# Moving the first turn of a 96-wide head from attention step 4 into step 5 of a hybrid decoder trunk

## The reference

```python
qb = heads(rms_norm(cq, cq_norm) @ w_uq, B_HEADS)
kv = heads(rms_norm(ckv, ckv_norm) @ w_ukv, B_HEADS)
k_nope, vb = jnp.split(kv, [B_NOPE_DIM], axis=-1)
kb = jnp.concatenate([k_nope, k_rope], axis=-1)
qb = rope_slice(rms_norm(qb, mla_qn), B_NOPE_DIM, B_ROPE_DIM, cos_b, sin_b)
kb = rope_slice(rms_norm(kb, mla_kn), B_NOPE_DIM, B_ROPE_DIM, cos_b, sin_b)
yb = causal_attention(qb, kb, vb)
...
merged = jax.nn.sigmoid(g_a) * (ya @ w_br_a) + jax.nn.sigmoid(g_b) * (yb @ w_br_b)
```

## Time and profile before

| | us |
|---|---|
| median of 3 runs | 1272.4 |
| lowest and highest run | 1271.33, 1274.69 |
| the profiled execution | 1271.69 |
| its span on the core | 1269.9 |
| TensorE busy | 1253.3 |
| VectorE busy | 436.7 |
| ScalarE busy | 381.2 |

### The profile page before, as it was taken

One profiled execution on the slowest core, in us unless ns is written; L12 is line 12 of the kernel. 1 busy time (PEld: TensorE's weight loads), 2 busy tenths in 40 slices (PEclk: granted clock), 3 DMA queues, 4 the chain that ended last, 5 costly groups with the idle time before them and its releaser, 6 DMA issues.

```text
span 1269.9 us, 29364 instructions
## 1 busy us (share of the span) xinstructions
PE 1253.3 (99%) x13480; PEld 890.9 (70%) x13480; DVE 436.7 (34%) x706; ACT 381.2 (30%) x650; POOL 101.0 (8%) x96
## 2 busy tenths in 40 slices
PE   9999999999999989999999999999999999999997
PEld 7877788888889868785555556655665666667666
DVE  5786666554356785652111101110111011101110
ACT  7587836434337678721000000000000000000000
POOL 0220000000001210000001002002001020020011
PEclk9999999999999999999999999999999999999999
DMA  8632535655446524499999999999999999999981
GB/s 300 211 106 100 199 133 185 229 184 197 149 139 227 173 67 166 160 381 424 421 423 422 408 422 402 422 423 394 422 419 404 423 403 417 423 398 423 417 336 16
DMA packets 77108, 379.95 MB, mean 299 GB/s; under 512 B 7786, under 2 KB 14612, under 8 KB 52404
## 3 DMA queue, kind: packets, MB, share of 16 engines
q1 hardware_dynamic: 71872, 369.99, 74.4%
q0 software_dynamic: 4464, 5.90, 2.2%
q10 hardware_dynamic: 644, 2.12, 0.4%
HBM read 372.75 MB, written 5.24 MB: 298 GB/s over the span
## 4 chain that ended last, share of the span: by engine, by line
PE 93%; DVE 3%; ACT 2%; issue 1%; DMA 1%; POOL 0%; DVEq 0%; POOLq 0%; ACTq 0%
PE ps L1205 36%; PE ps L1222 18%; PE ps L714 11%; PE ps L716 11%; PE ps L715 11%; ACT w_hi L1320 1%; PE ps L846 1%; PE ps L839 1%; PE ps L899 1%; DVE mix L1701 1%; DVE mix L1698 1%; ACT mix L1310 0%; PE ps L872 0%; ACT h_scaled L1388 0%; PE ps L835 0%
## 5 line engine op out<-in xcount | busy, mean ns | idle before, releaser
L1205 PE MATMUL ps<-s_unit,eT 128*32 128x352 f32 x4512 | 342.1, 459 | 0.0
L1205 PEld LDWEIGHTS ps<-s_unit,eT 128*32 128x32 f32 x4512 | 181.2, 110 | 147.5 <-issue 0.5
L1663 DVE TENSOR_TENSOR w_lo<-raw,w_hi 128x2048 fp32r<-128x2048 f32 (+3 forms) x93 | 197.1, 2125 | 110.4 <-ACT w_hi L1320 109.8
L1320 ACT CAST w_hi<-raw 128x2048 fp32r<-128x2048 f32 (+3 forms) x93 | 165.3, 1781 | 119.0 <-PE ps L716 105.5
L714 PE MATMUL ps<-w_hi,hT_hi 128*128 128x512 f32 (+1 forms) x464 | 180.9, 390 | 1.4 <-DVE w_lo L1934 0.9
L1606 ACT ACTIVATE e_act<-ps 128x352 f32<-128x352 f32 x48 | 22.2, 463 | 529.4 <-PE ps L1205 529.4
L716 PE MATMUL ps<-w_hi,hT_lo 128*128 128x512 f32 (+1 forms) x464 | 177.7, 383 | 0.0
L715 PE MATMUL ps<-w_lo,hT_hi 128*128 128x512 f32 (+1 forms) x464 | 177.4, 382 | 0.0
L1222 PE MATMUL ps<-s_unit,hidT 128*32 128x256 f32 x2244 | 133.6, 379 | 0.0
L2070 DVE TENSOR_TENSOR e_act<-e_act,ps 128x352 f32<-128x352 f32 x48 | 24.2, 504 | 314.7 <-ACT e_act L1606 313.3
L1205 PE MATMUL ps<-m_unit,eT 128*32 128x352 f32 x1632 | 124.3, 459 | 0.0
(11 more groups left out here) (196 smaller groups left out, 1143.9 us busy)
## 6 DMA issues: line engine op xcount, KB each, us to landing
s_unit<-in_experts_dram SPq DMA_DIRECT2D x128, 1408.0 KB, 15.8
m_unit<-in_experts_dram SPq DMA_DIRECT2D x64, 1408.0 KB, 15.3
raw<-in_w_in_dram SPq DMA_DIRECT2D x28, 1024.0 KB, 5.3
raw<-in_dense_w_gate_up_dram SPq DMA_DIRECT2D x20, 1024.0 KB, 5.2
raw<-in_dense_w_down_dram SPq DMA_DIRECT2D x9, 1024.0 KB, 5.0
raw<-in_w_out_dram SPq DMA_DIRECT2D x8, 1024.0 KB, 4.9
raw<-in_w_in_dram SPq DMA_DIRECT2D x8, 672.0 KB, 4.6
raw<-in_w_branch_a_dram SPq DMA_DIRECT2D x4, 1024.0 KB, 5.0
```

The costliest lines, as they stand in the source:

```text
L1205: last = pe.matmul(ps[2 * g + gu][strip(q), 0:PIECE], eT[:, g, STRIP * b:STRIP * (b + 1)], unit[:, at:at + PIECE], start=b == 0, stop=b == ...
L1320: act.copy(w_hi[u % SPLIT][:, 0:SIZE[u]], raw[u % RAW][:, 0:SIZE[u]]).then_inc(hi_ready, 1)
L1663: dve.tensor_tensor(w_lo[q][:, 0:m], raw[u % RAW][:, 0:m], w_hi[q][:, 0:m].bitcast(F32), ALU.subtract).then_inc(split, 1)
```

## The change

The turn of head 0 of branch B, in each layer, is issued in step 5 instead of step 4: behind the turned probabilities of head 5 and ahead of the gate products of step 5. Head 1's turn stays behind those gate products. The plan of the banks follows the new order, and ScalarE copies both heads in its step 5, one behind the other.

```diff
-B_TURNS = range(4, 12)
+B_TURNS = {5: (0, 1), **{k: (k - 4,) for k in range(6, 12)}}
...
-            if k in B_TURNS:
-                tile["bT", l, k - B_TURNS[0]] = banks.turns(4)
+            for hd in B_TURNS.get(k, ()):
+                tile["bT", l, hd] = banks.turns(4)
...
                 for k in range(16):
                     scores(scores_at(k))
                     turn_probs(k)
+                    for hd in B_TURNS.get(k, ())[:-1]:
+                        turn_b(hd)
                     gates(k)
-                    if k in B_TURNS:
-                        turn_b(k - B_TURNS[0])
+                    for hd in B_TURNS.get(k, ())[-1:]:
+                        turn_b(hd)
                     if k % 2:
                         values(k)
...
-                    if k in B_TURNS:
-                        hd = k - B_TURNS[0]
+                    for hd in B_TURNS.get(k, ()):
                         t_ = tile["bT", l, hd]
                         full(t_)
                         copy_out(qkT_b[0:B_DIM, hd, :], t_, ps[t_.bank][0:B_DIM, :])
```

## The result

The changed kernel takes 1274.77 us (median of 22 runs, 1272.13 to 1275.94) beside 1271.94 us for the kernel before (22 runs, 1270.91 to 1274.69). The ratio is 1.0015, with an interval of 1.0009 to 1.0022: slower by 0.15%, inside the 0.3% that the prediction called no change, but about four times its +0.04%. (The ratio goes with the means, 1274.39 and 1272.42 us.

A forecast was written before the change was run, and what follows sets the result against it. TensorE, busy 1253.3 of 1269.9 us, was taken as the bound. The fourth turn and late copy cost 0.23 us a layer; 2 x 0.23 = 0.46 us on 1272.4 gave near 1272.9 us, +0.04%, range 1270.0 to 1275.6.

The forecast's parts named there:

- Part 1: Head 5's three turned probabilities move into TensorE's idle hole after step 4's gate products: hidden, worth nothing by themselves.
- part 2: Head 0's four turns replace three behind the hole, still waiting for head 6's scores to be read: +0.11 us a layer.
- Part 3: ScalarE's later copy of head 0 makes TensorE wait 0.12 us at step 6's scores; 0.23 us a layer with the fourth turn.
- the 0.46 us: Forecast's total cost over both layers' attention, 2 x 0.23 us, from the fourth turn and the late copy.
- Part 4: On ScalarE, the weight cast and copy of turned values come earlier, no longer behind head 0's turn: taken as 0.
- Rival 1: Three turns in the hole keep TensorE at 2.4 GHz behind it: 1.7 us a layer less, 1269.5 us; chance 0.10.
- The third rival: Head 0's turn gets its bank early, gate products start 0.4 us earlier, late copy eats the gain: 1272.9; chance 0.04.
- Rival 2: In attention, a second stretch at clock 0.50: +1.7 us in a layer, 1274.6, or both, 1276.3; chance 0.08.
- Its own signs of being wrong: Head 0's turns at 98.4, step 6 scores after 105.6, or a time difference beyond what those stretches' clock levels explain.

## Why the prediction was right, and where its size was off

- **Part 1 and part 2 held.** Three turns at 97.88 behind the scaling, four at 100.02 with L1753 as releaser, 0.70 us after its start, as the probabilities before (99.21 - 98.51). The hidden and the exposed group changed places, and nothing was gained.
- **Part 3 held as a number and failed as a term of the sum.** The scores of step 6 start at 106.27, 105.46 on the scale of the trace before (less 0.81), as forecast, and 0.22 us a layer is there in both traces of the changed kernel (6.95 against 6.73). It was worked out against a kernel whose gate products of step 5 ran at 0.50, and then used for all executions. In over half of the executions of the kernel before the clock is up there, by their mean, and the same late copy costs 1.23 us a layer, as the traces with dummies show. The term that was mis-sized is the 0.46 us: 2.35 us in those.
- **Part 4 held** as far as it goes: the cast stands in the hole, and ScalarE waits 2.83 us for the inversion. What it freed became worth something only with the inversion moved.
- **Rival 1, the clock stays up, had a chance of 0.10, came in the profiled execution and, by the mean clock, in about half of all, and gave the wrong price.** It subtracted 3.4 us for the clock without asking what TensorE meets next. The third rival had the answer: the late copy would eat the gain. Applied to the first, it gives a changed kernel that gains nothing from its clock, beside a kernel before that gains 1.0 us a layer (7.49 - 6.48).
- **Rival 2, a longer fall, was looked for in the wrong place.** A further fall did come, 2.46 us, but in routing, some 100 us behind the second of the moved turns. The prediction priced the clock in attention alone.
- **Its own signs of being wrong.** The turns and the scores came where it put them. But it named 0.50 behind the hole in both layers, and the profiled execution has 1.00; and the difference of the two profiled times, 3.83 us, is more than the clock in those stretches explains, since 2.46 us lie in routing. By these two signs the forecast holds for one kind of execution only.
- **That the median lies inside the range is in part luck.** The upper end of 1275.6 was set to hold a second fall of the clock in one attention. What brought 1274.77 was a late copy at full clock and a fall in routing, and neither was in the sum.
- **The mean adds up roughly.** Half of the changed kernel's executions are of the kind that loses 4.2 us: the spans 1273.6 and 1269.4 of the changed kernel and of before with dummies differ by -0.40 at the start, 2.35 to routing, 2.47 in routing, -0.22 behind it. The other half lose nothing (0.996) or 0.9 us (0.994). That gives some 2.3 us, if both kernels had their kinds in the same shares, which they have only roughly; the means of all executions are 1274.34 and 1272.38, 1.96 us or 0.15% apart. Of the 0.9 at 0.994 the traces explain 0.45; for the rest there is no trace of the kernel before in that state, and it stays open. Why the share of kinds differs so between the kernels is not shown; for routing it is shown only that dummies in attention can change it.

## What to carry to other kernels

A profile is one execution. Where its clock changes in the stretch that you argue from, work the sum out once for each level, and ask of each what the engine waits for next. A step moved behind a wait on one engine drags its copy on another; look at what stands ahead of that copy in its new place and who holds it, here an inversion behind a 2.3 us weight split that had nothing to do with the head being copied. And an idle hole is worth filling with moved work only if the last wait in front of the next long stretch gets shorter: a free bank and an earlier inversion did that (distance 7.71 to 5.23 us), the move alone did not.

## What the runs showed of the hardware

The granted clock of one program differs between executions, by place and not only in the mean. With one and the same idle hole, the kernel before fell to 1.2 GHz behind it in both of its traces and, by its mean clock of 0.999, kept 2.4 GHz in others. (For the second there is no trace, but a mean of 0.999 has no room for two stretches like those in attention.) The changed kernel has traces of both, a granted clock of 1.00 and of 0.68 in the same stretch. With 1.5 us of dummy matmuls in the hole it stayed at 1.00 in the trace and, by the mean clock, in all of 11 executions. A change in one place is felt in another: with ten more dummies in each attention, a delay of 1.6 us in all, the clock was at 0.52 and 0.50 in routing, some 90 us behind the second of them; what decides it there stays open. In the kernel before a fall in one attention costs 1.0 us, in the changed kernel none; a fall in routing costs 2.5 us. The edit's own cost was put at 0.46 us.
